# The last feed forward of a four-layer backbone: four of the seven products of a set chained in one PSUM bank

## The chip, the cores and the metric

The kernel runs on one core of one Trainium2 chip. The metric is the device time of one execution in microseconds (us), as the median of several runs. The engines are TensorE (PE in the profile, PEld its weight loads), VectorE (DVE), ScalarE (ACT), GpSimd (POOL) and SyncE (SP, which issues the loads of weights).

## The reference

Four layers run over 640 tokens of width 1024: 512 latent tokens and 128 context tokens, with their own modulation. Each layer has a token mixer (latent attention, a bidirectional scan, pooling, and latent attention again), then a dense gated feed forward with 2816 hidden units:

```
def swiglu(h, wg, wu, wd):
    return (jax.nn.silu(h @ wg) * (h @ wu)) @ wd

fs = swiglu(modulate(ys, ms[3], ms[4]), ffn_wg[layer], ffn_wu[layer], ffn_wd[layer])
ys = layer_norm(ALPHA * ys + ms[5] * fs, ln_g[layer, 1], ln_b[layer, 1])
```

Everything is float32. The kernel splits each float32 operand into a high part (fp32r) and a low rest, and makes one product from three matmuls: high by high, low weights by high, high weights by low.

## The kernel before, in words

Activations lie with the channels on the partitions and the 640 tokens along the free dimension, in two halves of 320. The first three layers use a plain feed forward. The last layer (`seven`, one function for each engine) computes the gate and up projections with Strassen's idea in Winograd's form: a set takes the weights of 256 hidden units in the gate or the up matrix as 2 x 2 quarters A11, A12, A21, A22 of 512 channels by 128 units, the modulated input as 2 x 2 quarters (two halves of channels, two halves of tokens), and makes the four output quarters from seven products of quarters, in place of eight. A product is 4 channel tiles x 3 matmuls of 320 columns (L1391 to L1399). There are 20 sets, in groups of 6, 8 and 6; an even set gives gate quarters, the odd one behind it the up quarters for the same hidden units. After each group the down projection runs over that group's hidden units for all eight output columns (`down`, L1468), and VectorE adds it, gated, into x (L2895). Two of the 22 hidden tiles are done plainly ahead of the first set.

The order of each engine's work is written out by hand; engines wait for each other by counting semaphores.

- TensorE: product 0 into bank 4, product 1 into bank 5, 2 into 6, 3 into 7, product 4 added in bank 4, 5 added in bank 6, 6 added in bank 7 (L1404 to L1452). Before product 4 it waits for the copy of bank 4, before 5 and 6 for VectorE's evacuations.
- VectorE: the four sums of weight quarters of the next set into banks 0 to 3 (`weight_sums`, L3096 to L3101), then five evacuations of the set (u2 L3144, u3 L3147, and three corners L3132, L3134 or L3168), in between the low parts of the summed weights (`sum_low`, L3108), and for an odd set the gating multiplies (L3159, L3170, L3171). Ahead of the sets it forms the input's combinations (L3060 to L3066) and the two plain tiles' gating (`first_act`, L3072).
- ScalarE: the high parts of all weight operands (`high`, L2733), one copy of bank 4 after product 0 (L2774), the Silus (L2770, L2771, L2781), the high parts of the gated activations (`activated`, L2737).
- GpSimd: the low parts of the input's combinations (`turned_low`, L1139) and of the raw weight quarters (`low`, L1154).
- SyncE: weight chunks of 512 KB into a ring of four raw buffers; a buffer is loaded again when its low parts and sums are done (L830 to L858).

The high and low weight parts lie in a ring of eight half slots. An operand's cast waits for the product eight operands earlier. In this kernel the order of operands is that of the products, set by set (`set_operand`, `operand`, L237 to L262):

```
pe.wait_ge(s7.first, at.first + s + 1)
product(o + 4, 4, *plain(4, 0), False)
pe.wait_ge(s7.plo, at.plo + pool_lows(o + 5))
pe.wait_ge(s7.post, post + 2)
if s == 0:
    pe.wait_ge(s7.tlo, at.tlo + 3)
product(o + 5, 6, *mixed(3), False)
```

Of the kernel before, what the change touches and what calls it, by code (L numbers as in the profile page):

```python
# [217 lines left out]
LAST_LAYER = DEPTH - 1  # L218
SEVEN_FROM = LAYER_BASE[LAST_LAYER] + C_MIX[MIXER[LAST_LAYER]]
SEVEN_START = SEVEN_FROM + 4  # L220
# [4 lines left out]
PRODUCTS = 7  # L225
QUARTER = 4 * P
FROM_RAW = {0: 0, 4: 1, 5: 2}
SUM_SLOT = {1: 1, 2: 2, 3: 0, 6: 3}
SUM_LOW = {1: 0, 2: 1, 3: 2, 6: 3}
SUM_READ = {1: 4, 2: 2, 3: 3, 6: 4}  # L230
SEVEN_RAW = RAW + 1
OPERANDS = PRODUCTS * SETS + 2 * KD * GROUPS
# [5 lines left out]
def set_operand(s):  # L238


    return PRODUCTS * s + 2 * KD * group_of(s)

def down_operand(g, c):


    return PRODUCTS * GROUP_SETS[g + 1] + 2 * KD * g + 2 * c

def operand(o):


    for g in range(GROUPS):
        if o < down_operand(g, 0):
            s, j = divmod(o - set_operand(GROUP_SETS[g]), PRODUCTS)
            return "set", GROUP_SETS[g] + s, j
        if o < down_operand(g, KD):
            c, h = divmod(o - down_operand(g, 0), 2)
            return "down", (g, c), h

def pool_lows(o):


    kind, at, j = operand(o)  # L262
    if kind == "set":
        return 3 * at + 2 * KD * group_of(at) + FROM_RAW[j] + 1
    return 3 * GROUP_SETS[at[0] + 1] + 2 * KD * at[0] + 2 * at[1] + j + 1

def weight_slot(o):

    s = (2 * (SEVEN_START % RS) + o) % (2 * RS)
    return s // 2, s % 2 * QUARTER  # L270
# [9 lines left out]
def seven_chunks():  # L280


    def cut(first, t, n):
        while n:
            c, k = divmod(t, CH)
            m = min(n, CH - k)
            yield SEVEN_FROM + first + c, k, m
            t, n = t + m, n - m
# [3 lines left out]
    for g in range(GROUPS):  # L292
        for s in range(GROUP_SETS[g], GROUP_SETS[g + 1]):
            for f in (2 + s // 2 * 2, 3 + s // 2 * 2):
                c = 2 * f + s % 2 if f < first_half else 3 * first_half + 2 * (f - first_half) + s % 2
                order.append([(SEVEN_FROM + c, 0, CH)])
# [10 lines left out]
def seven_landed(r, order):  # L307

    return 16 * sum(len(order[n]) for n in range(r % SEVEN_RAW, r + 1, SEVEN_RAW))
# [33 lines left out]
def build(nc, a, o):  # L343
    ctx = ExitStack()
    with ctx:
# [98 lines left out]
        def f_seven(m, g):  # L444
            m.hhi, m.hlo = g("g_hhi", [P, KD, T], F32R), g("g_hlo", [P, KD, T], F32R)
            m.thi, m.tlo = g("g_thi", [P, 4, 4, HT], F32R), g("g_tlo", [P, 4, 4, HT], F32R)
            m.ahi, m.alo = g("g_ahi", [P, 8, T], F32R), g("g_alo", [P, 8, T], F32R)
            m.G, m.U = g("g_G", [P, 4, HT]), g("g_U", [P, 4, HT])
            m.p1, m.u2, m.u3 = g("g_p1", [P, HT]), g("g_u2", [P, HT]), g("g_u3", [P, HT])
            m.raw = g("g_raw", [P, CH * P])  # L450

        def f_seven_h(m, g):

            g("g_gap0", [P, 2 * KD * T + 2 * 16 * HT + 2 * T])
            m.h = [g("g_h0", [P, 4, T])]
            g("g_gap1", [P, 2 * T + 2 * T])
            m.h.append(g("g_h1", [P, 4, T]))

# [122 lines left out]
        m_ffn = [scope(f_ffn(L)) for L in range(LAST_LAYER)]  # L581
        m_seven, m_seven_h = scope(f_seven), scope(f_seven_h)
# [20 lines left out]
        def uses(tag, counts, n, primed=(), without=(None, ())):  # L603
# [13 lines left out]
        q_ffn = uses("ffn", dict(xa=KD, mm=NF, sil=NF, act=NF, hi=NF, lo=NF, down=2 * KD, upd=2 * KD), DEPTH)  # L617
# [11 lines left out]
        Seven = namedtuple("Seven", "gate thi tlo tsum hi plo dlo sum first post silu act prod")  # L629
        q_seven = Seven(gate=q_rwb.kys, thi=q_rwb.e0, tlo=q_rwb.til, tsum=q_rwb.prod, hi=q_rwb.r, plo=q_rwb.u, dlo=q_rwb.y, sum=q_rwb.sc,  # L630
                        first=q_rwb.first, post=q_rwb.msk, silu=q_rwb.bk, act=q_rwb.rev, prod=q_rwb.tk)
        seven_at = Seven(gate=PAIRS, thi=PAIRS, tlo=PAIRS, tsum=PAIRS, hi=10 * PAIRS, plo=10 * PAIRS, dlo=10 * PAIRS, sum=10 * PAIRS,
                         first=PAIRS, post=10 * PAIRS, silu=10 * PAIRS, act=10 * PAIRS, prod=10 * PAIRS)
        seven_land = [(q_rwb.ld, 64 * PAIRS), (q_rwb.ldr, 16 * PAIRS), (q_rwb.ldg, 16 * PAIRS), (q_rwb.ald, 16 * PAIRS)]

        def seven_raw(r):


            n = r % SEVEN_RAW
            return raw[:, (SEVEN_START + n) % RAW, :] if n < RAW else m_seven.raw[:, :]  # L640

# [26 lines left out]
        def _(sp):  # L668
# [9 lines left out]
            def stream(first, last):  # L678
                n = first
                while n < last:  # L680
                    loops = (last - n) // RAW
                    if n >= RAW and n % RAW == 0 and loops > 1:
                        with sp.Fori(0, loops) as i:
                            for u in range(RAW):
                                chunk(u, n, a["w"][i * RAW + (n + u)], i * RAW + (n + u - RAW + 1))
                        n += loops * RAW
                    else:
                        chunk(n % RAW, n, a["w"][n], n - RAW + 1 if n >= RAW else None)
                        n += 1

            def pieces(first, order, n0=0, n1=None):

                for n, runs in enumerate(order[n0:n1], first + n0):
# [3 lines left out]
                    for c, k0, count in runs:  # L697
                        sp.dma_start(raw[:, n % RAW, k * P:(k + count) * P], a["w"][first + c][:, k0 * P:(k0 + count) * P]
# [3 lines left out]
            def heads(L):  # L702
# [82 lines left out]
                order, first = rwkv_chunks(), LAYER_BASE[L]  # L785
# [44 lines left out]
            def seven(L):  # L830
                q, at = q_seven, seven_at

                def load(r, runs):
                    k = 0
                    for c, k0, count in runs:
                        sp.dma_start(seven_raw(r)[:, k * P:(k + count) * P], a["w"][c][:, k0 * P:(k0 + count) * P]
                                     ).then_inc(seven_land[r % SEVEN_RAW][0], 16)
                        k += count

                order = seven_chunks()  # L840
                for r in range(SEVEN_RAW):
                    if r < RAW:
                        sp.wait_ge(w_split, SEVEN_START - RAW + r + 1)
                    else:
                        sp.wait_ge(q_out[L].mm, q_out[L].at.mm + 1)
                    load(r, order[r])
                for g in range(GROUPS):
                    for s in range(GROUP_SETS[g], GROUP_SETS[g + 1]):
                        for n in range(2):
                            r = set_chunk(s) + n + SEVEN_RAW  # L850
                            if r < len(order):
                                sp.wait_ge(q.plo, at.plo + pool_lows(set_operand(s) + 4 + n))
                                sp.wait_ge(q.sum, at.sum + 4 * s + 4)
                                load(r, order[r])
                    for c in range(KD):
                        r = down_chunk(g, c) + SEVEN_RAW
                        if r < len(order):
                            sp.wait_ge(q.plo, at.plo + pool_lows(down_operand(g, c) + 1))  # L858
                            load(r, order[r])
# [38 lines left out]
            for L in range(DEPTH):  # L898
                if MIXER[L] == 1:
                    held = LAYER_BASE[L] + C_RWKV_LORA + C_RWKV_UP + C_RWKV_RKV + RAW  # L900
                    pieces(LAYER_BASE[L], rwkv_chunks(), 0, -2)
                    heads(L)
                    stream(held, LAYER_BASE[L + 1])
                elif L == 0:
# [22 lines left out]
                    stream(n + LATE_PAIR, LAYER_BASE[1])  # L927
                elif L == LAST_LAYER:
                    pieces(LAYER_BASE[L], [[(c, 0, CH)] for c in MLA_IN])
                    stream(LAYER_BASE[L] + C_MLA_IN, SEVEN_START)  # L930
                    seven(L)
                else:
                    stream(LAYER_BASE[L], LAYER_BASE[L + 1])
# [3 lines left out]
        def _(pool):  # L937
            def split(raw_slot, slot, land, used, n1):
                pool.wait_ge(w_land[raw_slot], land)
                if used is not None:  # L940
# [106 lines left out]
            def attention(L):  # L1047
                m, q = m_mla[L], q_mla[L]
                ch = late_chain
                chunk = LAYER_BASE[L] + HEADS_AT + HEADS_AHEAD  # L1050
# [49 lines left out]

            mixed = MIXER.index(1)
            heads_at = LAYER_BASE[mixed] + C_RWKV_LORA + C_RWKV_UP + C_RWKV_RKV
            stream(0, HEADS_AT + HEADS_AHEAD)
            attention(0)
            stream(HEADS_AT + HEADS_AHEAD + HEADS // 2, LAYER_BASE[mixed])
            landed, order = [0] * RAW, rwkv_chunks()

            def rwkv_pieces(n0, n1):

                for n, runs in enumerate(order[n0:n1], LAYER_BASE[mixed] + n0):  # L1110
# [10 lines left out]
            stream(heads_at + 2, LAYER_BASE[pooled] + RS)  # L1121
# [7 lines left out]
            stream(LAYER_BASE[pooled] + RS, LAYER_BASE[again] + HEADS_AT + HEADS_AHEAD)  # L1129
# [2828 lines left out]
```

## Time and profile before

| what | us |
|---|---|
| median of three runs | 3643.28 |
| lowest, highest | 3636.74, 3644.46 |
| the profiled execution, its own time | 3643.86 |
| its span, first to last instruction | 3642.1 |
| TensorE busy in it | 3347.9 (92%) |
| VectorE, ScalarE, GpSimd busy | 2463.9, 1046.3, 1819.6 |
| mean granted clock of TensorE | 0.974 |

The sets and the down parts lie from about 3202 us to the end of the span. A wait in the trace is idle time of an engine ahead of an instruction, with what released it. "issue" is idle time for which the trace shows no releaser. The chain of waits is read back from the last instruction.

### The profile page before, as it was taken

To read this page: it belongs to the slowest core of one execution; us is meant where nothing else is said; L and a number is where in the kernel's file an instruction comes from. 1 tells how busy PE (TensorE), PEld (TensorE's weight loads), DVE (VectorE), ACT (ScalarE), POOL (GpSimd) and SP (SyncE) were. 2 spreads that over 40 slices of the span, in tenths; PEclk is the share of its full clock that TensorE was granted. 3 is DMA by queue.
4 is the path that set the end of the run, shared out by engine and by line. 5 is a ranking of instruction groups with operands and counts; after the bars stand their busy time and mean duration, and the time that the engine had idled before them with its cause. 6 is when DMAs were issued, how large, how long until landed. Compare 5 with 4: busy or idle time off the path is not lost.

```text
span 3642.1 us, 72747 instructions
## 1 busy us (share of the span) xinstructions
PE 3347.9 (92%) x30644; PEld 3155.3 (87%) x30644; DVE 2463.9 (68%) x3554; ACT 1046.3 (29%) x2118; POOL 1819.6 (50%) x1441
## 2 busy tenths in 40 slices
PE   7888999999789778889999996999999999999997
PEld 5667899999789678888999995899998777899997
DVE  6666788787872567745875769885667565674556
ACT  4333231011353345542310013310013333252432
POOL 4585456565255655625565552565564222443322
PEclk9999999999899899999999997999999999999998
DMA  7111134443255444332343431344332000222221
GB/s 250 58 53 36 59 128 162 145 141 109 76 178 174 127 99 100 84 100 64 122 156 122 134 110 44 108 153 133 121 119 78 24 18 18 64 71 81 93 67 55
DMA packets 230318, 367.59 MB, mean 101 GB/s; under 512 B 105648, under 2 KB 113008, under 8 KB 229872
## 3 DMA queue, kind: packets, MB, share of 16 engines
q1 hardware_dynamic: 172752, 250.82, 22.9%
q10 hardware_dynamic: 57248, 112.18, 9.0%
q8 instruction: 242, 3.96, 0.4%
q14 instruction: 76, 0.62, 0.1%
HBM read 326.41 MB, written 36.54 MB: 100 GB/s over the span
## 4 chain that ended last, share of the span: by engine, by line
PE 75%; DVE 15%; ACT 3%; issue 3%; DMA 2%; SPq 1%; ACTq 0%; POOL 0%; DVEq 0%; POOLq 0%
PE ps L1184 47%; PE ps L1397 7%; PE ps L1468 4%; PE ps L1606 3%; PE ps L1253 2%; PE ps L1619 2%; PE ps L1637 2%; DVE x L2984 1%; PE ps L1578 1%; DVE m_mx L3292 1%; DVE ps L3537 1%; DVE x L2971 1%; DVE s_T L3536 1%; PE ps L1737 1%; DVE ln_cols L2944 1%
## 5 line engine op out<-in xcount | busy, mean ns | idle before, releaser
L943 POOL TENSOR_SCALAR w_hi<-w_raw 128x1024 fp32r<-128x1024 f32 x292 | 340.6, 1166 | 921.8 <-PE ps L1184 658.1
L2868 DVE SCALAR_TENSOR_TENSOR f_acc<-f_unit,silu_c,f_acc 128x512 f32<-128x512 f32 x532 | 614.4, 1195 | 8.2
L948 POOL TENSOR_TENSOR w_lo<-w_raw,w_hi 128x512 fp32r<-128x512 f32 x292 | 462.5, 1584 | 0.0
L1184 PE MATMUL ps<-f_hhi,w_hi 128*128 128x320 f32 x1968 | 448.5, 309 | 0.0
L1184 PE MATMUL ps<-f_hlo,w_hi 128*128 128x320 f32 x1968 | 448.4, 309 | 0.0
L1184 PE MATMUL ps<-f_hhi,w_lo 128*128 128x320 f32 x1968 | 448.2, 309 | 0.0
L946 POOL TENSOR_TENSOR w_lo<-w_raw,w_hi 128x512 fp32r<-128x512 f32 x292 | 425.3, 1456 | 24.4
L1184 PEld LDWEIGHTS ps<-f_hhi,w_lo 128*128 128x128 f32 x1968 | 329.2, 188 | 0.0
L1184 PEld LDWEIGHTS ps<-f_hhi,w_hi 128*128 128x128 f32 x1968 | 329.1, 188 | 0.0
L1184 PEld LDWEIGHTS ps<-f_hlo,w_hi 128*128 128x128 f32 x1968 | 328.9, 188 | 0.0
L2895 DVE SCALAR_TENSOR_TENSOR x<-ps,mod,x 128x320 f32<-128x320 f32 (+2 forms) x288 | 108.6, 433 | 282.7 <-PE ps L1184 186.4
L2175 ACT ACTIVATE f_sil<-ps 128x640 f32<-128x640 f32 x66 | 46.6, 705 | 832.0 <-PE ps L1184 832.0
L1184 PE MATMUL ps<-f_ahi,w_hi 128*128 128x320 f32 x1056 | 241.8, 310 | 0.0
L1184 PE MATMUL ps<-f_ahi,w_lo 128*128 128x320 f32 x1056 | 240.7, 309 | 0.0
L1184 PE MATMUL ps<-f_alo,w_hi 128*128 128x320 f32 x1056 | 240.4, 309 | 0.0
L1154 POOL TENSOR_TENSOR w_lo<-w_raw,w_hi 128x512 fp32r<-128x512 f32 (+1 forms) x86 | 112.5, 1313 | 221.1 <-ACT w_hi L2733 221.1
L1184 PEld LDWEIGHTS ps<-f_ahi,w_hi 128*128 128x128 f32 x1056 | 176.4, 188 | 1.4 <-issue 0.9
L1184 PEld LDWEIGHTS ps<-f_alo,w_hi 128*128 128x128 f32 x1056 | 176.7, 188 | 0.0
L1184 PEld LDWEIGHTS ps<-f_ahi,w_lo 128*128 128x128 f32 x1056 | 176.6, 188 | 0.0
L1606 PE MATMUL ps<-m_K,m_Q 128*128 128x320 f32 x512 | 163.4, 442 | 8.3 <-DVE m_Q L3278 8.3
L3020 DVE TENSOR_TENSOR f_a<-f_sil,ps 128x640 f32<-128x640 f32 x66 | 54.2, 821 | 172.2 <-ACT f_sil L2175 171.3
L2259 ACT ACTIVATE m_P<-ps,m_neg 128x640 f32<-128x640 f32 (+1 forms) x160 | 113.5, 710 | 183.8 <-DVE m_neg L3293 183.8
(504 smaller groups left out, 8241.6 us busy)
## 6 DMA issues: line engine op xcount, KB each, us to landing
w_raw<-in_w SPq DMA_DIRECT2D x312, 512.0 KB, 3.5
f_unit<-in_ada_w ACTq DMA_DIRECT2D x76, 1024.0 KB, 5.7
up_scratch<-r_o ACTq DMA_DIRECT2D x40, 320.0 KB, 2.5
ada_ring<-in_ada_w SPq DMA_DIRECT2D x8, 1024.0 KB, 6.6
late_step<-in_ada_w SPq DMA_DIRECT2D x32, 256.0 KB, 3.5
w_raw<-in_w SPq DMA_DIRECT2D x24, 256.0 KB, 3.0
s_LW<-up_scratch SPq DMA_DIRECT2D x16, 320.0 KB, 5.5
s_LA<-up_scratch SPq DMA_DIRECT2D x8, 640.0 KB, 7.3
```

Of the source, the lines that this page charges most:

```text
L943: nc.gpsimd.tensor_scalar(whi[:, slot, :], raw[:, raw_slot, :], 1.0, 0.0, ALU.mult, ALU.add).then_inc(w_hi_done, 1)
L946: nc.gpsimd.tensor_tensor(wlo[:, slot, 0:half], raw[:, raw_slot, 0:half], whi[:, slot, 0:half].bitcast(F32), ALU.subtract)
L948: nc.gpsimd.tensor_tensor(wlo[:, slot, half:], raw[:, raw_slot, half:], whi[:, slot, half:].bitcast(F32), ALU.subtract).then_inc(w_split, 1)
L1154: nc.gpsimd.tensor_tensor(wlo[:, s, c:c + width], src, whi[:, s, c:c + width].bitcast(F32), ALU.subtract).then_inc(q.plo, 1)
L1184: last = mm(ps[:, 2 * b + h, 0:HT], w, r[:, h * HT:(h + 1) * HT], start=kt == 0 and n < 2, stop=kt == KT - 1 and n >= 4)
L1253: last = mm(ps[:, 2 * p + h, 0:HT], w, r[:, h * HT:(h + 1) * HT], start=kt == 0 and n == 0, stop=kt == KD - 1 and n == 2)
L1397: last = mm(ps[:, bank, 0:HT], w, r, start=first and k == 0 and n == 0, stop=k == 3 and n == 2, skip_group_check=not first)
L1468: last = mm(ps[:, 2 * b + h, 0:HT], wt, r[:, k, h * HT:(h + 1) * HT], start=k == 0 and n < 2, stop=k == 2 * half - 1 and n >= 4)
L1606: last = mm(ps[:, b + h, 0:HT], query, m.K[:, hh, h * HT:(h + 1) * HT], start=True, stop=True)
L2259: af(dst, s, ACT.Exp, bias=m.neg[:, u % 2:u % 2 + 1], scale=SM_SCALE, accum_out=m.total[:, u:u + 1]).then_inc(q.pexp, 1)
L2868: last = stt(acc[:, cd, :], unit[:, k, :], by, acc[:, cd, :], ALU.mult, ALU.add)
L2895: last = stt(xs, ps[:, 2 * b + h, t0:t1], gate[:, c, cd:cd + 1], xs, ALU.mult, ALU.add)
```

## The change

The seven products of a set are put in another order, and four of them (0, 2, 4, 5) are chained in one bank, the corner: bank 4 for an even set, bank 7 for an odd one. Product 1 goes to bank 5, product 3 to bank 6, and product 6 is added in bank 6. The old fifth product is the new product 1 and takes raw weights; the old products 1 and 2 are the new 2 and 4. Product 0 of the next set of the same group is issued between products 4 and 5. ScalarE copies the corner after products 0, 2 and 4 into the set's result tiles, and TensorE waits for such a copy before it adds the next product to the bank. On ScalarE the copy after product 2 stands ahead of the casts of the next set's sums, the copy after product 4 behind three of them. VectorE adds bank 5 to the first copy, bank 6 to the third, and bank 6, after product 6, to the second; the fourth quarter is the corner itself after product 5. Signs are moved so that two input combinations and two gating multiplies use the three-operand form. The gating of an odd set is four multiplies of 320 columns. The order of weight operands follows the products; a look-up table replaces the arithmetic for their places. The modulated input is laid out by quarters. A refill of a set's first raw buffer waits for the low part of product 1.

Besides, the code is made able to serve other layers (chunk counting by a stream table, loads of modulation weights by halves for a following layer). The list of layers holds the last one only, so these parts issue nothing.

The diff is cut to its core; of the lines removed most are left out, since the section on the kernel before tells what they do.

```
-OPERANDS = PRODUCTS * SETS + 2 * KD * GROUPS
+def operand_order():
+    order = []
+    for g in range(GROUPS):
+        sets = range(GROUP_SETS[g], GROUP_SETS[g + 1])
+        order.append((sets[0], 0))
+        for s in sets:
+            order += [(s, 1), (s, 2), (s, 3), (s, 4)]
+            if s + 1 in sets:
+                order.append((s + 1, 0))
+            order += [(s, 5), (s, 6)]
+        order += [(("down", g, c), h) for c in range(KD) for h in range(2)]
+    return order
...
@@ GpSimd @@
                 low(0)
+                low(1)
                 turned_low(3, 4)
...
@@ TensorE @@
+                def seven_set(s, g):
+                    opening, more = s == GROUP_SETS[g], s + 1 < GROUP_SETS[g + 1]
+                    if opening:
+                        if s == 0:
+                            pe.wait_ge(q.sil, q.at.sil + 2)
+                        else:
+                            pe.wait_ge(q.upd, q.at.upd + KD * g - 1)
+                        product(s, 0, corner(s), *plain(0, 0), True)
+                    else:
+                        pe.wait_ge(s7.post, at.post + 3 * s - 2)
                     if s == 0:
                         pe.wait_ge(q.act, q.at.act + 2)
                     elif opening:
                         pe.wait_ge(q.upd, q.at.upd + KD * g)
+                    product(s, 1, 5, *plain(1, 0), True)
+                    if s == 0:
+                        pe.wait_ge(s7.tsum, at.tsum + 5)
+                    pe.wait_ge(s7.copied, at.copied + 3 * s + 1)
+                    product(s, 2, corner(s), *mixed(0), False)
                     if s == 0:
                         pe.wait_ge(s7.tlo, at.tlo + 2)
+                    if not opening:
+                        pe.wait_ge(s7.post, at.post + 3 * s)
+                    product(s, 3, 6, *mixed(2), True)
+                    pe.wait_ge(s7.copied, at.copied + 3 * s + 2)
+                    product(s, 4, corner(s), *mixed(1), False)
+                    if more:
...
+                        product(s + 1, 0, corner(s + 1), *plain(0, 0), True)
...
+                    pe.wait_ge(s7.copied, at.copied + 3 * s + 3)
+                    product(s, 5, corner(s), *mixed(3), False)
+                    pe.wait_ge(s7.post, at.post + 3 * s + 2)
+                    product(s, 6, 6, *plain(1, 1), False)
...
@@ ScalarE, one set @@
+                        if opening:
+                            corner_copied(s, 0)
+                            after(0)
                         if not gated:
+                            act.wait_ge(s7.post, at.post + 3 * s)
+                            af(m.G[:, 0:2, :], m.G[:, 0:2, :], ACT.Silu).then_inc(s7.silu, 1)
                         if gated and not opening:
+                            pair_activated(s // 2 - 1)
+                        corner_copied(s, 2)
+                        after(1)
+                        after(2)
+                        after(3)
+                        corner_copied(s, 4)
+                        after(4)
+                        if more:
+                            corner_copied(s + 1, 0)
+                            after(0, s + 1)
                         if gated:
+                            act.wait_ge(s7.prod, at.prod + OPERAND_AT[s, 5] + 1)
+                            af(m.G[:, 2, :], ps[:, 4, 0:HT], ACT.Silu, scale=-1.0).then_inc(s7.silu, 1)
+                            act.wait_ge(s7.post, at.post + 3 * s + 2)
+                            af(m.G[:, 3, :], m.G[:, 3, :], ACT.Silu, scale=-1.0).then_inc(s7.silu, 1)
+                        after(5)
+                        after(6)
...
@@ VectorE @@
-                tt(t2, t3, t2, ALU.add).then_inc(s7.tsum, 1)
+                stt(t2, t3, -1.0, t2, ALU.mult, ALU.subtract).then_inc(s7.tsum, 1)
...
-                tt(t4, t2, t4, ALU.subtract).then_inc(s7.tsum, 1)
+                stt(t4, t2, -1.0, t4, ALU.mult, ALU.subtract).then_inc(s7.tsum, 1)
...
+                        tt(D[:, 0, :], D[:, 0, :], ps[:, 5, 0:HT], ALU.add).then_inc(s7.post, 1)
+                        if not gated_set:
...
+                            tt(U[:, 0, :], U[:, 0, :], G[:, 0, :], ALU.mult).then_inc(s7.act, 1)
                         if more:
                             sum_low(s + 1, 2)
+                            sum_low(s + 1, 3)
...
+                        dve.wait_ge(s7.copied, at.copied + 3 * s + 3)
+                        tt(D[:, 3, :], D[:, 3, :], ps[:, 6, 0:HT], ALU.add).then_inc(s7.post, 1)
...
+                            stt(U[:, 3, :], U[:, 3, :], -1.0, G[:, 3, :], ALU.mult, ALU.mult).then_inc(s7.act, 1)
                         if more:
+                            sum_low(s + 1, 4)
                         if not gated_set:
+                            done(5)
+                            stt(U[:, 2, :], ps[:, 7, 0:HT], -1.0, G[:, 2, :], ALU.mult, ALU.mult).then_inc(s7.act, 1)
                         if more:
                             sum_low(s + 1, 6)
+                        done(6)
+                        tt(D[:, 1, :], D[:, 1, :], ps[:, 6, 0:HT], ALU.add).then_inc(s7.post, 1)
+                        if not gated_set:
...
+                            tt(U[:, 1, :], U[:, 1, :], G[:, 1, :], ALU.mult).then_inc(s7.act, 1)
```

Here `corner(s)` is bank 7 for an odd set and bank 4 for an even one; `after(j)` casts the operand eight places behind product j of the set; `corner_copied(s, j)` waits for product j and copies the corner; `done(j)` waits for product j.

## Rows read from the trace of the kernel before

**Rows 1.** The page: the span and the number of instructions.
```profile
span 3642.1 us, 72747 instructions
```

**Rows 2.** Chain of waits from 3150 us on: start us, us, what.
```profile
3218.46 65.35 PE ps L1397 x444
...
3340.13 98.56 PE ps L1397 x672
...
3495.01 73.92 PE ps L1397 x504
...
3591.23 1.15 DVE x L2895 x3
...
3615.63 4.53 PE ps L1296 x20
```

**Rows 3.** TensorE's waits, 2950 us to the end: total, times, longest us.
```profile
PE ps L1397 <- DVE w_lo L3108: 4.6, 1, 4.6
...
PE ps L1397 <- issue: 0.9, 1, 0.9
```

**Rows 4.** Windows: us; busy PE, PEld, DVE, ACT, POOL; granted clock; DMA share; GB/s.
```profile
3209.00:3212.00 3.00, 3.00 (x12) 3.00 (x13) 2.61 (x5) 2.47 (x5) 1.14 (x1) 0.50 0.00 0
...
3340.00:3439.00 99.00, 99.00 (x677) 99.00 (x677) 68.83 (x116) 44.89 (x82) 36.91 (x28) 1.00 0.28 87
```

**Rows 5.** Groups by line, 2900 us to the end: busy us, mean ns, idle before.
```profile
L2733 ACT CAST w_hi<-ps 128x512 fp32r<-128x512 f32 x80 | 43.9, 591 | 78.8 <-DVE ps L3101 45.7 <-PE ps L1397 22.9 <-PE ps L1468 10.2
...
L3144 DVE TENSOR_TENSOR g_u<-g_p,ps 128x320 f32<-128x320 f32 x20 | 9.7, 484 | 13.2 <-PE ps L1397 13.2
...
L2774 ACT COPY g_p<-ps 128x320 f32<-128x320 f32 x20 | 8.4, 422 | 9.6 <-PE ps L1397 9.6
...
L1154 POOL TENSOR_TENSOR w_lo<-w_raw,w_hi 128x512 fp32r<-128x512 f32 x74 | 100.3, 1359 | 207.5 <-ACT w_hi L2733 207.5
```

**Rows 6.** Timeline of one set in the middle: start us, us, instruction, idle before.
```profile
3366.22 0.31 PE L1397 MATMUL ps<-g_hlo,w_hi 128*128 128x320 f32 x1
...
3366.57 0.43 ACT L2774 COPY g_p<-ps 128x320 f32<-128x320 f32 x1 [1.14 <-PE ps L1397]
...
3367.60 0.69 DVE L3096 TENSOR_TENSOR ps<-g_raw 128x512 f32<-128x512 f32 x1
...
3369.52 0.69 DVE L3101 TENSOR_TENSOR ps<-w_raw,ps 128x512 f32<-128x512 f32 x1
...
3370.31 1.56 ACT L2733 CAST w_hi<-ps 128x512 fp32r<-128x512 f32 x3 [1.87 <-DVE ps L3101]
```

**Rows 7.** Two lines of VectorE: ns min/median/max, first and last start us.
```profile
L2868 DVE SCALAR_TENSOR_TENSOR f_acc<-f_unit,silu_c,f_acc x532: 737/753/1798, 493.9 to 2724.5; 128x512 f32<-128x512 f32 x178
...
L3096 DVE TENSOR_TENSOR ps<-g_raw x10: 684/693/1807, 3212.6 to 3547.1; 128x512 f32<-128x512 f32 x10
```

**Rows 8.** Timeline at TensorE's second stop: VectorE's evacuation, then TensorE.
```profile
3217.87 0.49 DVE L3147 TENSOR_TENSOR g_u<-g_u,ps 128x320 f32<-128x320 f32 x1
...
3218.46 0.38 PE L1397 MATMUL ps<-g_thi,w_hi 128*128 128x320 f32 x1 [0.90 <-issue]
3218.68 0.31 PE L1397 MATMUL ps<-g_thi,w_lo 128*128 128x320 f32 x1
```

**Rows 9.** VectorE's timeline over the opening of the first set.
```profile
3195.47 4.14 DVE L3066 TENSOR_TENSOR g_h<-g_h 128x1280 f32<-128x1280 f32 x1
...
3205.95 1.49 DVE L3113 TENSOR_TENSOR g_tlo<-g_h,g_thi 128x1280 fp32r<-128x1280 f32 x1
...
3208.69 0.81 DVE L3072 TENSOR_TENSOR g_U<-g_G,ps 128x640 f32<-128x640 f32 x1
```

**Rows 10.** GpSimd's timeline over the same stretch.
```profile
3191.11 7.16 POOL L1139 TENSOR_TENSOR g_tlo<-g_h,g_thi 128x1280 fp32r<-128x1280 f32 x2 [13.43 <-ACT g_thi L2709]
3198.23 2.56 POOL L1154 TENSOR_TENSOR w_lo<-w_raw,w_hi 128x512 fp32r<-128x512 f32 x1
```

**Rows 11.** ScalarE's timeline over the same stretch: the copy after product 0.
```profile
3212.21 0.42 ACT L2774 COPY g_p<-ps 128x320 f32<-128x320 f32 x1
```

More of the change, by code:

```diff
@@ L286, in cut @@
             m = min(n, CH - k)
-            yield SEVEN_FROM + first + c, k, m
+            yield start + first + c, k, m
             t, n = t + m, n - m
@@ L457, in f_seven_h, with f_seven_ada @@
             m.h.append(g("g_h1", [P, 4, T]))
+        def f_seven_ada(m, g):
+            g("g_gap2", [P, 8 * HT])
+            m.half, m.part = [], []
+            for i in range(2):
+                m.half.append(g(f"g_half{i}", [P, 2, 512]))
+                m.part.append(g(f"g_part{i}", [P, 6 * 32]))
+                if i == 0:
+                    g("g_gap3", [P, 4 * HT - 2 * 512 - 6 * 32])
         def f_ln(t):
@@ L632, in build @@
[L632 to L636, printed above, removed]
-            n = r % SEVEN_RAW
-            return raw[:, (SEVEN_START + n) % RAW, :] if n < RAW else m_seven.raw[:, :]
+                        copied=q_rwb.first, post=q_rwb.msk, silu=q_rwb.bk, act=q_rwb.rev, prod=q_rwb.tk)
@@ L678, in stream @@
             def stream(first, last):
-                n = first
+                n, gap = first, source(first)
                 while n < last:
@@ L1394, in product @@
                     for k in range(4):
-                        wh, wl = whi[:, s, c + k * P:c + (k + 1) * P], wlo[:, s, c + k * P:c + (k + 1) * P]
-                        for n, (w, r) in enumerate(((wh, bhi(k)), (wl, bhi(k)), (wh, blo(k)))):
-                            last = mm(ps[:, bank, 0:HT], w, r, start=first and k == 0 and n == 0, stop=k == 3 and n == 2,
+                        wh, wl = whi[:, w, c + k * P:c + (k + 1) * P], wlo[:, w, c + k * P:c + (k + 1) * P]
+                        for n, (wt, r) in enumerate(((wh, high(k)), (wl, high(k)), (wh, low(k)))):
+                            last = mm(ps[:, bank, 0:HT], wt, r, start=first and k == 0 and n == 0, stop=k == 3 and n == 2,
@@ new lines, in down @@
+                    width, o = tiles // 2, down_operand(g, c)
+                    for n, k in enumerate((*range(tiles - 2), tiles - 1, tiles - 2)):
+                        if n % width == 0:
+                            pe.wait_ge(s7.plo, at.plo + POOL_LOWS[o + n // width])
+                        late = c == 0 and n >= tiles - 2
+                        s, col = weight_slot(L, o + k // width)
+                        w = [t[:, s, col + k % width * P:col + (k % width + 1) * P] for t in (whi, wlo)]
@@ new lines, in half_sums @@
+                def half_sums():
+                    pe.wait_ge(unit_red, RED_BASE[L] + ADA_UNITS // 2)
+                    for i in range(2):
+                        part = m_seven_ada.part[i][:, :].rearrange("p (c d t r) -> p c t d r", c=6, d=2, r=4)
+                        for r in range(4):
+                            last = mm(ps[32 * r:32 * r + 32, 2, HT + 48 * i:HT + 48 * i + 48], pick[:, :], part[:, :, :, :, r], start=True, stop=True)
+                    last.then_inc(unit_sum, 1)
@@ L2739, in pair_activated @@
[L2739 to L2746 removed]
+                        act.wait_ge(*seven_land(L, raw_chunk(o)))
+                        weight, width = seven_weight(L, o)
+                    s, c = weight_slot(L, o)
+                    nc.scalar.copy(whi[:, s, c:c + width], weight).then_inc(s7.hi, 1)
```

581 lines of the change are left out of this document (309 added, 272 removed).

## The prediction

> **What bounds the kernel now.** I read the page's span first [rows 1], then the chain of waits in order of time over the last 500 us [rows 2], because everything ahead of the last feed forward is the same program: the diff only renames how weight chunks are counted there, and its new waits and loads are off for the last layer. The reader should see that from 3218.46 to 3591 us the chain is TensorE alone: 65.35 us for 444 matmuls, 98.56 for 672, 73.92 for 504, each 0.1467 us a matmul and without a piece of another engine between. A product is 12 matmuls, so 1.76 us, a set of seven 12.3 us. Only with the fourth output column of the last group, at 3591, does the chain pass to VectorE's sums and then to the last layer norm; that tail hangs on the matmuls ahead of it and moves with them. The waits of TensorE [rows 3] give all that it lost among the products: 4.6 us once, ahead of the second product of the first set, and 0.9 us once. The window behind the first wait shows a third loss [rows 4]: the granted clock was 0.50 (1.2 GHz) after the gap, so that some 12 matmuls took about 3.3 us in place of 1.76, 1.5 lost. So 4.6 + 0.9 + 1.5 = 7.0 us is all that better waiting can win ahead of the tail; the number of matmuls stays at 1680 for the products and 1056 for the down part.
>
> **The work that is traded.** Each set loses two VectorE evacuations (five become three): 40 x 0.484 us [rows 5] = 19 us less VectorE. It gains two ScalarE copies (one becomes three): 40 x 0.422 us = 17 us more ScalarE. The gating multiplies become four of 320 columns in place of two and one of 640, the Silus keep their count and widths, GpSimd keeps its 108 subtractions. In the middle group, 99 us of TensorE, VectorE is busy 68.83 and ScalarE 44.89 [rows 4]. So I price all of this at nothing by itself: its cover is the TensorE row, and it costs something only where one copy comes later than the product that waits for it. That is what has to be looked at, in three places.
>
> **A set in the middle.** I count from the start of product 1; the order is 1, 2, 3, 4, 0 of the next set, 5, 6, at 0, 1.76, 3.52, 5.28, 7.04, 8.80 and 10.56. A copy starts 0.04 after the last matmul ends (3366.22 + 0.31 to 3366.57) and takes 0.43 [rows 6]. Product 4 needs the copy after product 2: 3.56 to 4.0, with ScalarE free, since that copy stands ahead of the casts; needed at 5.28. Behind it on ScalarE stand three casts of the next set's sums, and behind these the copy after product 4, which product 5 needs at 8.80. VectorE ends the previous set at about 1.05 (two instructions of 0.49 behind product 6 [rows 8]), and its four sums take 2.6 (the fourth starts 1.92 behind the first and lasts 0.69), so 3.7; the casts are 1.56 [rows 6], the third cannot start before product 3 has ended at 5.3, so ScalarE is free at 5.9. Product 4 ends at 7.04, its copy at 7.5, 1.3 us early. The sums could be 3.0 us later (6.7, + 1.56 + 0.43 = 8.7) before TensorE waits. The largest blocked sum in this stage took 1.807 against a median of 0.693 [rows 7]; two such add 2.2, still 0.8 short. Product 6 needs the sum with product 3, one VectorE instruction behind the 7.5 copy: about 8.5 against 10.56. Product 3 needs bank 6 read out by the previous set: 0.6 against 3.52. So **a middle set costs nothing**.
>
> **The end of a group.** The last set of a group has no next product 0, so product 5 follows product 4 and stands in the same bank behind its copy. Nothing hides that: 0.31 - 0.15 for the end of the last matmul, 0.04, 0.43 for the copy, then the restart. A restart is in the trace: a VectorE result at 3217.87 + 0.49 lets a matmul start at 3218.46, 0.10 later, and the next follows after 0.22 in place of 0.15 [rows 8], 0.07 more. Together 0.16 + 0.04 + 0.43 + 0.10 + 0.07 = 0.8 us, three times: **+2.4 us**. The ends are 0.5 (copy alone) and 1.2 (behind one more cast of 0.59 [rows 5]), so 1.5 to 3.6. The gap of 0.90 did not lower the clock, and this one is no longer. The down part's first column has cover: its last tile is now gated by one 320-column multiply, shorter than the 640 before.
>
> **The opening of a group.** Product 1 waits for the eighth output column to be gated: 1.15 us of VectorE [rows 2] and some 0.2 of passing on, against product 0's 1.76. Nothing, with 0.4 to spare; ends 0 and 0.5 each for the two later groups.
>
> **The first set.** Product 1 now needs raw weights and the second gating multiply (it stands behind that wait in TensorE's order), where product 1 needed a sum's low part before. That multiply ended at 3208.69 + 0.81 = 3209.50 [rows 9], 0.7 us behind the old start. What moves it: GpSimd now makes one more low part ahead of its third long subtraction. The rows show that VectorE and GpSimd keep each other out when VectorE reads two tensors from SBUF: the 128x1280 instruction issued at 3195.47 took 4.14, and ended 1.34 behind the GpSimd pair that ended at 3191.11 + 7.16 = 3198.27; the low part issued at 3198.23 then took 2.56, where the mean is 1.36 [rows 5, 9, 10]. They alternate. By the same order the first weight sum goes at 3200.79, the new low part at 3201.34 to 3202.5, the second sum to 3203.1, the third long subtraction 2.85 (as the second of the pair behind 3195.43) to 3205.9, and VectorE's own long one (3205.95 before) ends at about 3207.3 in place of 3207.4. So the multiply ends at 3209.4, product 1 starts at 3209.45, +0.6; ends -0.5 and +2.0 (GpSimd first at 3200.79 adds some 1.4). It again runs at the low clock, 3.3 us, to 3212.75; the copy after product 0 stood at 3212.21 behind the same four casts [rows 11] and is ready then. The 0.90 gap before product 5 has no releaser in the trace; in the code product 5 waits for the second evacuation, which ended at 3218.36, late because it stood behind the next set's weight sums, and 0.10 ahead of the restart [rows 8]. That wait is gone. In its place product 5 (at 3219.8) waits for the copy behind three casts: weight sums end at 3218.1 by my count, + 0.05 + 1.56 + 0.43 = 3220.1, 0.3 late. So 0.6 - 0.9 + 0.3 = **0.0**, ends -1.2 and +2.5.
>
> Two of the four combinations of input quarters change from a plain subtract or add to the three-operand form, both on that opening path. The trace has no such form at 1280 columns; at 512 with two SBUF inputs its shortest is 0.737 and its median 0.753 [rows 7], against 0.693 for a plain add [rows 7]: I take +0.05 each, inside the 0.0, and keep up to doubling as the other end. The Trainium skill, in Vector Engine (DVE) Microarchitecture Reference, section Points that are easy to get wrong, says that this form with two SBUF inputs wider than bf16 runs at half speed; by that the sum would be some 3 us higher, and the 512-column rows speak against it.
>
> SP's loads: the first refill waits for the low part of product 1, not of the old fifth product, so it goes at about 3204.5 in place of 3212.6 on idle queues. It costs nothing.
>
> **The sum.** The profiled execution took 3643.86 us, its span 3642.1 [rows 1]; 3643.86 + 0.0 + 2.4 = 3646.3. The median of the three runs is 0.6 lower, 3643.28, so the forecast is **3645.7 us**. With the ends -1.2 + 1.5 and +2.5 + 3.6 + 1.0 that is 3643.6 to 3650.4. The runs before went from 3636.74 to 3644.46; about 0.2% (7.3 us) is what a measurement of this kernel can tell from no change.
>
> **Rivals.**
> *ScalarE becomes the gate of every set* (slower). Place: the copy after product 4, behind three casts that wait for VectorE's sums. It decides once the sums slip by over 3.0 us; for it: in the first set they nearly do. Against: 30% of VectorE's time and over half of ScalarE's are free [rows 4]. At 3.5 us of slip, 0.5 x 17 sets = 8.5, 3654. Chance 0.09.
> *The opening gets shorter.* If the three-operand form is not kept out by GpSimd, its two instructions cost about 1.5 each, not 4.14: VectorE is ready up to 5.2 us earlier. ScalarE's first Silu feeds the same multiply, so I allow 4 of it (a choice), and 1.5 with the clock kept: 3645.7 - 5.5 = 3640. For it: nothing in rows; against: the three-operand rows reach 1.798 where the median is 0.753 [rows 7], as blocked ones do. Chance 0.08.
> *The three-operand form doubles.* 2 x 1.45 on the opening path, 3648.7. Chance 0.05.
> *The chained bank costs nothing at the ends*, as if the copies were covered: 3643.3. Chance 0.12.
>
> **How the numbers follow.** The forecast keeps 0.64, the rivals 0.34, and 0.02 stays for what I did not see. Faster by over 0.2% means below 3636.0, more than all 7.0 us that waits can give: 0.05, mostly for a lower set of runs. Slower means above 3650.6: the first rival, and 0.04 of the unseen and of the upper ends, 0.13. No difference: 0.82. The range reaches down through the shorter opening with 2 us of scatter and up to the worst sum of ends: 3638 to 3652.
>
> **What would show it.** Right: matmul counts unchanged; one gap of about 0.8 us before product 5 of sets 5, 13 and 19, none in the others; the chain from the second set to 3591 TensorE alone; the gap behind the first product 5.4 us, followed by half clock. Wrong: TensorE waits on ScalarE's copies in most sets; the two three-operand instructions at 1.5 us or near 5.5; a gap of VectorE's sums into the next set; VectorE no less busy.

## The result, and the profile after

Changed kernel: median 3650.67 us (19 runs, 3640.9 to 3655.48); kernel before on the same chip: 3643.28 (19 runs, 3636.04 to 3648.02). The ratio is 1.0020, interval 1.0013 to 1.0028. A second series, of 12 runs, gave 3645.46 against 3643.73, ratio 1.0008, 0.9997 to 1.0019. So the change makes the kernel slower by between nothing and 0.3%, about what a measurement can tell. The profiled execution took 3653.15 us, 9.3 more than that of before. One run of the last experiment, e_best, took 4871.87 us at a mean granted clock of 0.63, where its other eleven took 3637.08 to 3648.59 us at 0.969 to 0.974; it is left out of the comparison there.

Most of those 9.3 us arise ahead of the stage that was changed. I cut each profiled execution at one point, the end of the last out projection (the chain's row of 288 matmuls, its start and length added): ahead of it all kernels issue the same instructions, behind it lies the changed stage. The row in before, then in after:

```profile
3117.90 42.25 PE ps L1184 x288
```

```profile
3124.26 42.25 PE ps L1270 x288
```

The times from it to the end of the span (spans are given to 0.1 us):

| profiled execution | out projection ends | span | changed stage |
|---|---|---|---|
| before | 3160.15 | 3642.1 | 481.95 |
| after | 3166.51 | 3651.4 | 484.89 |
| before, again | 3162.32 | 3643.8 | 481.48 |
| after, again | 3157.47 | 3642.1 | 484.63 |

The stage grew by 2.94 and 3.15 us. The part ahead of it came out 6.4 us later in one pair and 4.9 earlier in the other. In the first pair it comes from the second layer's scan: the instructions of after stand 2.7 us ahead of those of before at 1252 us, and 6.2 behind them at 1656. The window from 1400 to 1500 us, in which 2.9 of these us arise, before and then after (stretch; its us, PE busy, matmuls; granted clock; DMA share; GB/s):

```profile
1400.00:1500.00 100.00, 85.80 (x2609) 1.00 0.42 101
```

```profile
1400.00:1500.00 100.00, 86.92 (x2514) 0.95 0.41 100
```

The reader should see a granted clock 0.05 lower in after, with 95 fewer matmuls in the same time, and this in a stage that the diff leaves alone. In the next 100 us, in which 3.4 more arise, it is 0.93 against 0.95. That the clock is the cause, and not another sign of the same delay, was not shown.

Now the changed stage. The chain of waits of after (start us, us, what), which answers to [rows 2]:

```profile
3215.71 71.64 PE ps L1487 x468
3287.37 0.43 ACT g_U L2859
...
3287.84 3.78 PE ps L1487 x24
...
3347.95 95.05 PE ps L1487 x648
3443.02 0.44 ACT g_U L2859
...
3443.50 3.78 PE ps L1487 x24
...
3503.60 70.41 PE ps L1487 x480
3574.04 0.43 ACT g_U L2859
...
3574.52 3.78 PE ps L1487 x24
```

The chain was TensorE alone from the second set on. Now a ScalarE copy stands in it three times, 24 matmuls (products 5 and 6) ahead of the end of each group. The middle group's sets, 3347.95 to 3447.28, take 99.33 us in place of 98.56; the last, 3503.60 to 3578.30, 74.70 in place of 73.92: +0.77 and +0.78. TensorE's waits from 2950 us on, those on the products (total, times, longest us), answer to [rows 3]:

```profile
PE ps L1487 <- DVE g_U L3207: 5.1, 1, 5.1
...
PE ps L1487 <- ACT g_U L2859: 1.5, 3, 0.5
```

Two lines are all: one gap ahead of product 1 of the first set, now behind a gating multiply, and three waits on the copy. In the other 17 sets TensorE waits for no copy.

The timeline at the first group's end, as TensorE and ScalarE see it (start us, us, instruction, idle before):

```profile
3287.02 0.31 PE L1487 MATMUL ps<-g_tlo,w_hi 128*128 128x320 f32 x1
3287.37 0.43 ACT L2859 COPY g_U<-ps 128x320 f32<-128x320 f32 x1 [1.14 <-PE ps L1487]
...
3287.84 0.41 PE L1487 MATMUL ps<-g_thi,w_hi 128*128 128x320 f32 x1 [0.52 <-ACT g_U L2859]
```

The last matmul of product 4 starts at 3287.02 and ends at 3287.33, the copy ends at 3287.80, and product 5 starts at 3287.84.

The granted clock at the opening, and the middle group, taken like that of before over its first 99 us (columns as in [rows 4]):

```profile
3215.71:3221.74 6.03, 6.03 (x22) 6.03 (x23) 5.22 (x6) 3.56 (x7) 4.25 (x3) 0.50 0.06 5
...
3348.00:3447.00 99.00, 98.48 (x672) 98.22 (x671) 65.55 (x104) 50.29 (x98) 37.59 (x27) 1.00 0.29 91
```

The clock is 0.50 for 6 us behind the gap, over 22 matmuls, where before it was 11, from 3208.83 to 3211.93. In the middle group VectorE is busy 65.55 in place of 68.83 and ScalarE 50.29 in place of 44.89.

### The profile page after: what moved, and what is told of

The parts are those of the page before. It is cut to its first block, busy times and chain, and to the rows that moved or that the text cites. A ratio compares the mean times of both kernels' runs of the same rounds, so it can differ in the third digit from the quotient of the medians.

```text
span 3651.4 us, 72754 instructions
## 1 busy us (share of the span) xinstructions
PE 3364.3 (92%) x30644; PEld 3170.2 (87%) x30644; DVE 2457.1 (67%) x3524; ACT 1061.4 (29%) x2158; POOL 1827.6 (50%) x1441
## 4 chain that ended last, share of the span: by engine, by line
PE 75%; DVE 14%; ACT 3%; issue 3%; DMA 2%; SPq 1%; ACTq 0%; POOL 0%; DVEq 0%; POOLq 0%
PE ps L1270 46%; PE ps L1487 7%; PE ps L1552 4%; PE ps L1699 3%; PE ps L1339 2%; PE ps L1712 2%; PE ps L1730 2%; DVE x L3115 1%; PE ps L1671 1%; DVE m_mx L3450 1%; DVE x L3102 1%; DVE ps L3695 1%; DMA inv_scratch<-s_L 1%; DVE s_T L3694 1%; DVE ln_cols L3075 1%
```

## The experiments

Two questions were open. The first: is what came on top of the stage's 3 us scatter of the scan (theory A in the expectations), or does it belong to the changed program (theory B)? The second: are the stage's own 3 us the three uncovered copies, and is it the place of a copy or its amount that counts? Times below are the changed stage's, as in the table, since the scatter ahead of it is larger than any of these edits.

**Controls.** Both kernels again, without an edit.

> The kernel before once more, unchanged, as a control. The changed kernel's median was 7.4 us above the one before, but in the two traces only 2.9 us of the difference lies behind the out projection of the last layer; 6.4 us arose between 1250 and 1663 us, in the scan of the second layer, whose instructions are the same. Theory A (the scan scatters from execution to execution): this control also lands up to 5 us off the kernel before, either way, and its scan ends anywhere within 6 us. Theory B (the rest belongs to the changed program): this control lands within 1 us of the kernel before.

> The changed kernel once more, unchanged. Theory A: +3 us against the kernel before, give or take 3. Theory B: +7 us again. In both, the stretch from the end of the out projection to the end of the span is 484.9 us as in its first trace, 2.9 above the kernel before.

Measured: the kernel before against itself, 3646.73 (12 runs) against 3643.73 (29 runs), ratio 1.0007, 0.9995 to 1.0019; the kernel after, 1.0008, 0.9997 to 1.0019. The stages were 481.48 and 484.63. TensorE's waits on the products in the kernel before, this time, and the window behind the wait:

```profile
PE ps L1397 <- DVE w_lo L3108: 4.7, 1, 4.7
```

```profile
3211.03:3217.03 6.00, 6.00 (x22) 0.50 0.19 44
```

The same kernel lies 3.0 us above itself, no less than the changed one (1.7), while the stage repeats within 0.5, and the shift ahead of the stage did not come back. So the executions fit A, and B's "within 1 us" and "+7 again" both failed. The medians leave some room: the second series' interval reaches 1.0019 and the first begins at 1.0013, where the stage's 3 us are 0.0008, so a small shift of the changed program's own is not excluded. The control also corrects the reading of before: the gap of 0.90 in [rows 3] is not there, and the low clock behind the 4.7 lasted 22 matmuls, 3211.03 to 3217.03, not 11. One loss stands in for the other: behind the longer low clock, product 5 comes too late to have to wait.

**The closing sets in another order (e_order).** In sets 5, 13 and 19 products 2 and 4 go ahead of 1 and 3, so that another product lies between a copy and the product that needs it.

```diff
-                    product(s, 1, 5, *plain(1, 0), True)
+                    if more:
+                        product(s, 1, 5, *plain(1, 0), True)
                     product(s, 2, corner(s), *mixed(0), False)
+                    if not more:
+                        product(s, 1, 5, *plain(1, 0), True)
...
                     product(s, 4, corner(s), *mixed(1), False)
+                    if not more:
+                        product(s, 3, 6, *mixed(2), True)
```

(with the same for the copy after product 4, ahead of the third cast, and the counters.)

> The changed kernel with the last set of each group in the order 2, 1, 4, 3, 5, 6, so that product 1 or 3 lies behind every copy that a chained product waits for. If the three gaps of 0.78 us before product 5 of sets 5, 13 and 19 are the copy's latency with nothing to cover it: the gaps vanish, and the stretch from the out projection to the end is 2.3 us shorter than in the changed kernel, 482.6 us. If the gaps come from VectorE's or ScalarE's queue being behind at a group's end: gaps of 0.3 us or more remain before products 5 or 6.

Measured: stage 481.73, 2.9 and 3.2 under the two of after; total 3646.27 (12 runs), ratio to before 1.0007, 0.9996 to 1.0019. The chain, and TensorE's only wait on the products:

```profile
3351.24 98.56 PE ps L1491 x672
...
3506.12 73.92 PE ps L1491 x504
```

```profile
PE ps L1491 <- DVE g_U L3228: 5.1, 1, 5.1
```

Both groups are back at 98.56 and 73.92, and no wait on ScalarE is left. That is the 2.3 us of the copies. Of the other 0.6 to 0.8, some 0.5 lies in the tail (from the end of the last group's sets to the end of the span), 72.56 in place of 73.10. It is none of the edit's, since the kernel before shows 73.17 in one execution and 72.56 in the other. The two values follow the granted clock at the start of the last layer norm's 20 matmuls. The first 2.4 us from there, in before and in before again:

```profile
3615.63:3618.03 2.40, 2.40 (x11) 0.50 0.00 0
```

```profile
3617.95:3620.35 2.40, 2.40 (x19) 1.00 0.00 0
```

Over the nine profiled executions the tail is 73.1 to 73.2 in the six in which the first ten of these matmuls ran at the low level (2.4 us), and 72.5 to 72.6 in the three in which all or nearly all of them ran at the full one (1.3 to 1.5 us): before again, e_order and e_best.

**The copy after product 2 behind the casts (e_late).** The rule that the change follows, undone for one copy; no work is added or taken.

```diff
-                        corner_copied(s, 2)
                         after(1)
                         after(2)
                         after(3)
+                        corner_copied(s, 2)
                         corner_copied(s, 4)
```

> The changed kernel with the copy after product 2 moved behind the three casts of the next set's sums, beside the copy after product 4. By the schedule counted for a middle set (ScalarE free of the third cast at 5.9 us, product 4 due at 5.28, copy 0.43, restart 0.17): product 4 waits about 1.2 us in each of 20 sets, and the kernel is 20 to 25 us slower than the changed one. If ScalarE has the slack that its 45% of busy time suggests: no more than 3 us.

Measured: stage 515.07, +30.2; total 3677.38 (4 runs), ratio to before 1.0098, 1.0078 to 1.0117. TensorE's waits, and the chain over one set:

```profile
PE ps L1487 <- ACT g_G L2859: 14.5, 10, 2.3
PE ps L1487 <- ACT g_U L2859: 12.0, 13, 1.1
```

```profile
3227.91 0.69 DVE ps L3234
...
3228.61 1.71 DVE ps L3235
...
3232.22 1.08 ACT w_hi L2824 x2
3233.30 0.34 ACT g_U L2859
...
3233.68 12.60 PE ps L1487 x84
```

TensorE now waits 23 times, up to 2.3 us, 26.5 in all. The chain tells why: VectorE's sums, ScalarE's casts of them, then the copy, then the products. ScalarE has no more to do than in after: 49.2 us in the middle group, which now takes 111, in place of 50.3 in 99. So what lies free on an engine says nothing here; the place in its order does. I expected 1.2 us in each set. The middle sets lost 1.2 and 1.6 in turn, restart included, and the first set 2.5. One of the four sums takes 1.8 us in most sets (1.71 on the chain above) where I counted 0.69; how much of the excess that makes was not separated.

**The opening: product 1 ahead of the wait (e_first).** In the first set only, product 1 no longer stands behind the second gating multiply (product 3 does), the set's copies go ahead of casts on ScalarE, and VectorE adds bank 5 to the first quarter ahead of the next set's sums, and bank 6 to the last between them.

```diff
-                    if s == 0:
-                        pe.wait_ge(q.act, q.at.act + 2)
-                    elif opening:
+                    if opening and s:
                         pe.wait_ge(q.upd, q.at.upd + KD * g)
                     product(s, 1, 5, *plain(1, 0), True)
...
                     if s == 0:
                         pe.wait_ge(s7.tlo, at.tlo + 2)
+                        pe.wait_ge(q.act, q.at.act + 2)
```

> The changed kernel with product 1 of the first set ahead of the wait for the second gating multiply (the wait stands before product 3, the first to use that multiply's bank), the first set's three copies ahead of casts that it does not need, and VectorE's first two additions for the set around its next sums. If product 1 stood idle only for that wait: it starts with no gap behind product 0, the gap is 2.8 us, before product 2, product 2 starts about 4 us earlier, and the stretch from the out projection to the end is 480 to 482 us (484.8 in the changed kernel). If VectorE's opening chain decides whatever the order: within 1 us of 484.8.

Measured (one execution): stage 480.97. TensorE's waits on the products, and the window behind the first:

```profile
PE ps L1487 <- DVE w_lo L3255: 2.7, 1, 2.7
PE ps L1487 <- ACT g_U L2858: 1.5, 3, 0.5
PE ps L1487 <- DVE g_G L3341: 0.8, 1, 0.8
```

```profile
3209.00:3215.00 6.00, 5.81 (x40) 5.84 (x41) 4.53 (x8) 3.90 (x8) 2.70 (x3) 1.00 0.02 3
```

One wait of 5.1 became 2.7 and 0.8, and the clock stayed at 1.00: 3.7 to 3.9 us less than after, with the three closing waits of 0.5 still in it.

**GpSimd held back from VectorE's combinations (e_wait).** GpSimd starts its long subtractions only when all four combinations are there.

```diff
+                pool.wait_ge(q.tsum, at.tsum + 4)
                 turned_low(1, 1)
```

> The changed kernel with one wait more: GpSimd's three long subtractions start only when VectorE has made all four input combinations. If the two engines keep each other out: the two three-operand instructions drop from 4.15 us to about 1.5 each, and give 5.3 us back; but by the same rule the later instructions are blocked in their place (two weight sums, the long VectorE subtraction, the activation's low part), so product 1 starts within 1.5 us of where it did and the stretch is 484 to 487 us. If the 4.15 us belong to the three-operand form or to its width: they stay at 4.15.

Measured (one execution): stage 485.25. VectorE's timeline, and TensorE's first wait:

```profile
3188.76 1.49 DVE L3196 TENSOR_TENSOR g_h<-g_h 128x1280 f32<-128x1280 f32 x1
...
3191.81 1.49 DVE L3200 SCALAR_TENSOR_TENSOR g_h<-g_h 128x1280 f32<-128x1280 f32 x1
...
3193.34 1.49 DVE L3202 SCALAR_TENSOR_TENSOR g_h<-g_h 128x1280 f32<-128x1280 f32 x1
...
3198.35 3.46 DVE L3236 TENSOR_TENSOR ps<-w_raw 128x512 f32<-128x512 f32 x1
...
3205.49 3.50 DVE L3213 TENSOR_TENSOR g_alo<-g_U,g_ahi 128x640 fp32r<-128x640 f32 x1
```

```profile
PE ps L1488 <- DVE g_U L3208: 5.3, 1, 5.3
```

Both three-operand instructions take 1.49, as the plain one above them. The gain does not reach TensorE: now a weight sum takes 3.46 (1.80 in after) and a low part 3.50 (0.81 in after), both beside GpSimd's long subtractions and ahead of the gating multiply. The wait is 5.3, and the stage no shorter.

**Together (e_best).** Three of the edits above (e_order, e_first, e_wait), and the low part that stood in the way moved behind two of the sums' low parts and the second gating multiply:

```diff
-                act_low(0, 0)
                 sum_low(0, 2)
...
                 sum_low(0, 3)
+                act_low(0, 0)
```

> e_order, e_first and e_wait together, and VectorE's low part of the first activation moved behind the first summed low parts and the second gating multiply. Counted with the durations of the traces: product 2 starts at about 46 us from the end of the out projection in place of 52.4, with next to no gap, so the clock stays full, and the three closing gaps are gone: a stretch of 475 to 478 us, 7 to 10 below the changed kernel, 4 to 6 below the kernel before. If VectorE then holds up the first two sets instead: 479 to 482. The total scatters more than that: a ratio between 0.997 and 1.001.

Measured: stage 475.96, 8.9 and 8.7 under the two of after, 6.0 and 5.5 under the two of before. TensorE's waits on the products, and the window that answers to the slow one of [rows 4]:

```profile
PE ps L1492 <- DVE g_G L3362: 0.8, 1, 0.8
...
PE ps L1492 <- POOL w_lo L1201: 0.2, 1, 0.2
```

```profile
3211.00:3214.00 3.00, 3.00 (x22) 3.00 (x21) 3.00 (x5) 2.12 (x5) 1.78 (x1) 1.00 0.16 63
```

One us of waiting is left of after's 6.6, all at the full clock. Of the gain on after, e_order's and e_first's edits gave 2.3 and 3.7 to 3.9 by themselves and the tail's clock 0.6; some 2 us are left for GpSimd's wait and the moved low part, which were not run apart. The total does not tell the kernel apart from before: ratio 0.9994, interval 0.9985 to 1.0004 (11 runs). The 5.5 to 6.0 us that the stage gains are 0.15 to 0.16% of the time, at the lower end of that interval, and 0.6 of the 6.0 are the tail's clock. So this version beats both kernels in the stage, in one execution, and is not shown to beat that of before in the whole.

## Why the prediction was right, and where not

- **Result.** The forecast was +2.4 us, and the stage gave +2.9 and +3.2. The pieces add up: in the first pair 2.3 for the copies, 0.7 for the first set and -0.1 for the tail; in the second 2.3, 0.2 and 0.6, the 0.6 being the tail's clock, which is luck and not the change. The second series' median, 3645.46, lies on the forecast. The first's, 3650.67, lies 5 us above it: inside the stated 3638 to 3652, but over the sum of the upper ends, 3650.4, and just over the 3650.6 at which the prediction begins to say slower. For the profiled execution the table puts that excess ahead of the stage. That it is so for the whole first series was not shown: its interval begins at 1.0013, and 3 us are 0.0008.
- **The end of a group.** Forecast 0.8 three times, behind product 4 of sets 5, 13 and 19 and nowhere else; measured 0.77 and 0.78 on the groups, in those three places, and gone in e_order. The sum of the pieces of [rows 6, 8] was the right price for a row that the trace of before did not have, if with a little luck: the restart came 0.04 behind the copy, not 0.10, and the matmul after it 0.26 later, not 0.22.
- **A set in the middle costs nothing.** Right: no wait in 17 sets, although the sums took longer than I gave them. The means of the two rows below rose from 1019 and 969 ns to 1503 and 1583. Groups by line (count, busy us, mean ns, idle before), before and then after:

```profile
L3096 DVE TENSOR_TENSOR ps<-g_raw 128x512 f32<-128x512 f32 x10 | 10.2, 1019 | 0.4
...
L3097 DVE TENSOR_TENSOR ps<-w_raw 128x512 f32<-128x512 f32 x10 | 9.7, 969 | 0.0
```

```profile
L3234 DVE TENSOR_TENSOR ps<-g_raw 128x512 f32<-128x512 f32 x10 | 15.0, 1503 | 0.4
...
L3235 DVE TENSOR_TENSOR ps<-w_raw 128x512 f32<-128x512 f32 x10 | 15.8, 1583 | 0.0
```

- **The work that is traded.** ScalarE got 17 us more in copies, as forecast: 60 copies of 428 ns, 25.6 us, in place of 8.4 [rows 5]. VectorE did not get 19 us lighter: 2457.1 us in place of 2463.9, 6.8 less. The 40 evacuations are gone, but the two rows above took 4.8 and 6.1 us more, so 11 of the 19 went into longer sums. "VectorE no less busy" was on my list of what would show the working wrong; it came half true and cost nothing.
- **The opening.** VectorE's and GpSimd's timelines of after, which answer to [rows 9, 10]:

```profile
3197.69 4.14 DVE L3199 SCALAR_TENSOR_TENSOR g_h<-g_h 128x1280 f32<-128x1280 f32 x1
3201.87 4.15 DVE L3201 SCALAR_TENSOR_TENSOR g_h<-g_h 128x1280 f32<-128x1280 f32 x1
...
3207.67 1.80 DVE L3235 TENSOR_TENSOR ps<-w_raw 128x512 f32<-128x512 f32 x1
```

```profile
3197.51 7.17 POOL L1189 TENSOR_TENSOR g_tlo<-g_h,g_thi 128x1280 fp32r<-128x1280 f32 x2 [13.45 <-ACT g_thi L2806]
...
3208.88 3.36 POOL L1189 TENSOR_TENSOR g_tlo<-g_h,g_thi 128x1280 fp32r<-128x1280 f32 x1
```

  The turns came as counted: shifted by the 6.36 us between the two out projections, the count has the second weight sum end at 3209.46 and the third long subtraction at 3212.26, and they ended at 3209.47 and 3212.24. The combination ends at 3206.02, 1.34 behind GpSimd's pair at 3204.68, as in before, and the three-operand form takes 4.15 where the plain one took 4.14. Product 1 started 49.20 us behind the out projection in place of 48.68: +0.52, forecast +0.62. The rival by which the form doubles falls. The Trainium skill, Vector Engine (DVE) Microarchitecture Reference, section Points that are easy to get wrong, has this form at half throughput for two SBUF sources that are not bf16. If that is meant against the plain form, the trace of e_wait disagrees, with 1.49 us for either form where GpSimd is held back.
- **The step that failed: the first set at 0.0.** I took the 0.90 of [rows 3] as a fixed price that the change removes, and the 3.3 us at the low clock as fixed and unchanged. The wait for the second evacuation did go. But the low clock lasted 22 matmuls and 6.0 us, 2.8 lost against 0.1467 each, not 11 and 1.5. It also covered the 0.3 that I had counted for the copy in its place, as the copy after product 4 and the start of product 5 in after show:

```profile
3225.82 0.43 ACT L2859 COPY g_G<-ps 128x320 f32<-128x320 f32 x1
```

```profile
3227.33 0.31 PE L1487 MATMUL ps<-g_thi,w_hi 128*128 128x320 f32 x1
```

  The copy ended 1.1 us ahead of product 5, which the longer low clock had put 1.3 later; so with the shorter one TensorE would have waited 0.2 to 0.3 (an estimate from these rows). From product 1 to the first down part after took 75.92 us, before 74.98; less the closing 0.78, and with the later start of 0.52, the first set cost +0.7. In the second pair (75.65 against 75.09, start +0.43) it cost +0.2. So 0.2 to 0.7 in place of 0.0. In the first pair that is the later start and the longer low clock, 1.3, less the 0.90 and its restart; in the second, where the low level lasted 20 and 22 matmuls and before had no second wait, it is the later start less some 0.2. How long the low clock lasts differs between executions of one kernel, so neither it nor the 0.90 behind it was a fixed term.
- **The rivals.** ScalarE as the gate of every set: not in after. e_late brings it about by the copy's place rather than by later sums, at 30 us, three and a half times my 8.5. The chained bank for nothing: e_order shows that a different order of the closing sets gives just that. The opening that gets shorter when the form is not kept out by GpSimd: its condition is false, since the form takes 4.15 beside GpSimd. e_wait gave the two instructions their 1.49 by holding GpSimd back, which is not quite that condition, and the opening stayed as long. My 4 us were counted on VectorE's two instructions alone; in e_wait the blocked time only moves.

## What to carry to other kernels

Where an engine off the bound works on the bound's behalf, look at what stands ahead of each result in its order, not at its busy share: one copy moved behind three casts cost 30 us on an engine that is busy for half of the middle group. A chain in one bank needs other products between its links; at the end of a group none is left behind the usual order, so give the closing sets an order of their own. Before a total is explained, cut the span at the last point where both programs are the same, and run the kernel before again: here the part that nobody touched moved by 4.9 and 6.4 us, where the change cost 3.

## What was not expected of the hardware

- **Scatter without an edit.** Over the nine profiled executions of this case the same instructions ahead of the stage ended between 3157.47 and 3170.87 us. The mean granted clock goes with it only roughly (0.974 in the two earliest, 0.969 and 0.970 in the two latest), and what starts a slower course stays open.
- **The clock behind a gap.** Gaps of 4.6 to 5.3 us ahead of a product were followed by the low level, a granted clock of 0.50 (1.2 of 2.4 GHz), for 11 to 22 matmuls; a gap of 2.7 us was not, nor were the waits of 0.5 to 0.9. So e_first, which took 1.6 us off a wait of 5.1, saved 3.7 to 3.9 us of the stage.
- **Turns.** Where VectorE and GpSimd both read two tensors from SBUF, a VectorE instruction of 1.49 us took 4.15 and ended 1.34 behind GpSimd's pair. Holding GpSimd back (e_wait) moved the blocked time to later instructions, 3.46 and 3.50 us, rather than saving it.
